# The HGRN scan stage rebuilt: block decays as one number each, values with channels on partitions, the root from a logarithm, and mem's attention moved among the value tiles

## The reference, cut to what matters

```python
q = silu(q); v = i                                   # 8 heads of 128
f = lb + (1 - lb) * sigmoid(z);  log_f = log(f);  k = 1 - f      # for zf and for zb
o = gla_chunked(q, k_f, v, lf_f) + flip(gla_chunked(flip(q), flip(k_b), flip(v), flip(lf_b)))
o = rmsnorm(o, norm_g.reshape(8, 128)) * silu(gate)
return concatenate([o, memory_cross_attn(xq, mem_kv)]) @ w_out
# gla: out[t] = sum over s <= t of (q[t] . (k[s] * exp(sum of log_f over s+1..t))) v[s]
```

## Time and profile before

| what | us |
|---|---|
| median of 3 runs (lowest to highest) | 1550.86 (1549.63 to 1552.31) |
| the profiled execution's own time | 1549.63 |
| its span in the trace | 1548.3 |
| HGRN stage in it, from PE's first value matmul (1074.04) to ACT's first step of the norm behind it (1338.55) | 264.5 |
| PE busy over the span | 1451.5 |
| DVE, ACT, POOL busy over the span | 984.0, 724.6, 206.2 |

### The profile page before, as it was taken

The page is one execution under the profiler, slowest core; times in us unless marked ns, Lnnn a source line. Parts: engine busy times, 40 slices in busy tenths (PEclk is TensorE's granted clock), DMA queues, the critical chain, the costliest instruction groups (busy, mean ns, idle before and its releaser), DMA issues.

```text
span 1548.3 us, 23402 instructions
## 1 busy us (share of the span) xinstructions
PE 1451.5 (94%) x9687; PEld 1282.6 (83%) x9687; DVE 984.0 (64%) x1697; ACT 724.6 (47%) x1041; POOL 206.2 (13%) x170
## 2 busy tenths in 40 slices
PE   7899999999999999999999999999987847799998
PEld 5887799999977999977667999996986746699997
DVE  5754576767756766673561666555599986365555
ACT  4434255554523554534453544454565643454443
POOL 2661300000000000027225000000000132400000
PEclk8999999999989999999999999999989858999999
DMA  8322155554442655525123456553532221355551
GB/s 306 139 101 109 55 218 191 215 184 180 191 163 104 222 191 218 191 109 184 62 82 109 168 186 218 191 182 140 198 124 93 82 96 41 136 191 181 193 194 73
DMA packets 36570, 240.42 MB, mean 155 GB/s; under 512 B 3880, under 2 KB 6256, under 8 KB 8944
## 3 DMA queue, kind: packets, MB, share of 16 engines
q1 hardware_dynamic: 36464, 238.92, 42.6%
HBM read 236.27 MB, written 2.64 MB: 154 GB/s over the span
## 4 chain that ended last, share of the span: by engine, by line
PE 80%; DVE 11%; ACT 5%; POOL 2%; issue 1%; DMA 0%; SPq 0%; DVEq 0%; ACTq 0%
PE ps L356 23%; PE ps L323 14%; PE ps L324 14%; PE ps L325 14%; DVE wlo L280 2%; PE ps L478 2%; PE ps L485 2%; POOL wlo L273 1%; DVE gb L1916 1%; PE ps L1568 1%; ACT whi L265 1%; PE ps L807 1%; PE ps L1582 1%; ACT gb L1825 1%; DVE ar L1953 1%
## 5 line engine op out<-in xcount | busy, mean ns | idle before, releaser
L323 PE MATMUL ps<-XS,whi 128*128 128x256 f32 x2088 | 603.6, 289 | 15.3 <-DVE XS L531 4.9
L324 PE MATMUL ps<-XS,whi 128*128 128x256 f32 x2088 | 599.1, 287 | 0.0
L325 PE MATMUL ps<-XS,wlo 128*128 128x256 f32 x2088 | 598.3, 287 | 0.0
L280 DVE TENSOR_TENSOR wlo<-raw,whi 128x2048 fp32r<-128x2048 f32 x168 | 383.8, 2287 | 162.0 <-ACT whi L265 161.8
L265 ACT ACTIVATE whi<-raw 128x2048 fp32r<-128x2048 f32 x204 | 388.5, 1907 | 136.4 <-PE ps L356 98.3
L323 PEld LDWEIGHTS ps<-XS,whi 128*128 128x128 f32 x2088 | 410.1, 196 | 21.4 <-issue 10.3
L324 PEld LDWEIGHTS ps<-XS,whi 128*128 128x128 f32 x2088 | 409.9, 196 | 1.6 <-issue 0.2
L325 PEld LDWEIGHTS ps<-XS,wlo 128*128 128x128 f32 x2088 | 409.2, 196 | 0.0
L356 PE MATMUL ps<-whi,MS 128*128 128x512 f32 x1024 | 291.0, 391 | 5.8 <-POOL wlo L273 5.2
L273 POOL TENSOR_TENSOR wlo<-raw,whi 128x512 fp32r<-128x512 f32 x142 | 189.3, 1367 | 587.3 <-ACT whi L265 587.3
L356 PEld LDWEIGHTS ps<-whi,MS 128*128 128x128 f32 x1024 | 189.2, 188 | 46.0 <-POOL wlo L273 6.4
(11 more groups left out here) (248 smaller groups left out, 1432.7 us busy)
## 6 DMA issues: line engine op xcount, KB each, us to landing
raw<-in_up SPq DMA_DIRECT2D x88, 1024.0 KB, 4.8
raw<-in_down SPq DMA_DIRECT2D x44, 1024.0 KB, 4.8
raw<-in_hg_t SPq DMA_DIRECT2D x16, 1024.0 KB, 4.8
raw<-in_od_t SPq DMA_DIRECT2D x8, 1024.0 KB, 5.0
raw<-in_ev_a SPq DMA_DIRECT2D x7, 1024.0 KB, 8.2
raw<-in_wa_o SPq DMA_DIRECT2D x6, 1024.0 KB, 4.8
raw<-in_hg_o SPq DMA_DIRECT2D x6, 1024.0 KB, 4.8
raw<-in_ev_o SPq DMA_DIRECT2D x4, 1024.0 KB, 7.1
```

The lines of the kernel that those rows point to most:

```text
L280: ve.tensor_tensor(lo[:, 0:w], r[:, 0:w], hi[:, 0:w].bitcast(F32), ALU.subtract).then_inc(w_lo_v)
L323: pe.matmul(d, hi[:, c], S[:, k, 0:256], start=(k == 0), stop=False)
L324: pe.matmul(d, hi[:, c], S[:, k, 256:512], start=False, stop=False)
L325: last = pe.matmul(d, lo[:, c], S[:, k, 0:256], start=False, stop=(k == 7))
```

## The change

Every part of it is in the HGRN stage.

- **Decays.** Only the 32-blocks keep their own exponentials: DVE takes two scans that restart at each block (`M32`, `CS`), one reduction for the sum of log f over each block, one scan of these 16 sums and four small subtractions that give one number for each block and level (`AA`, 48 columns). One subtraction of 512 columns makes `DD`. ACT takes exp(DD), exp(-DD) and exp(AA). The factors of the coarser levels are the factors of the 32-blocks times one number for each block (`X1_`, `X2_`, `X3_`).
- **Gates.** The logarithm takes scale and bias in the ACT instruction (`lf` straight from `SZ`), and k is not formed: a second sigmoid with the sign turned (`SN`) times a column.
- **Values** come with channels on partitions: two matmuls of 256 columns. ACT squares them, PE sums over partitions by a matmul with ones (`squares_pe`), ACT takes exp(-0.5 ln(.)) (`root_act`), DVE multiplies. Newton, the scaling, the turn on PE and the accumulated squares go.
- **Mem's attention** moves to the front: its query tiles come second and third, and its steps stand between the value tiles and the first heads. Its probabilities now lie in `gb`.
- **Low parts.** POOL makes every second `hg_t` tile (q and gate), `hg_x`, and `hg_o` tiles 0, 2 and 4. DVE makes the z tiles, `hg_v` and `hg_o` 1, 3 and 5.
- **Output.** The order is `hg_o` 4, 5 (mem's rows), 0, 1, 2, 3. The first four stand inside iterations 8 and 9.
- **Loop.** It runs over n from 0 to 10: projections of head n, factors of head n-1, values of head n-2, root of head n-3.

```diff
@@ tiles
-    add("hg_v", 4, ends=[1, 1, 1, 2])
+    add("hg_v", 1)
+    add("hg_x", 2)
+    add("hg_v", 3, at=1, ends=[1, 1, 2], key="hg_w")
     add("hg_t", 16)
-    add("hg_x", 2)
-    add("hg_o", 6, ends=[1, 1, 1, 1, 0, 4])
+    add("hg_o", 2, at=4)
+    add("hg_o", 4, ends=[1, 1, 0, 4], key="hg_p")
@@ who makes the low part
-POOLT = [_t[0] in ("ev_v", "ev_b", "ev_c", "ev_o", "hg_x", "hg_o") or _t[0][:2] == "wa"
-         or (_t[0] == "ev_a" and _t[1] > 1) for _t in SCHED]
+POOLT = [_t[0] in ("ev_v", "ev_b", "ev_c", "ev_o", "hg_x") or _t[0][:2] == "wa"
+         or (_t[0] == "ev_a" and _t[1] > 1) or (_t[0] == "hg_t" and _t[1] % 2 == 1)
+         or (_t[0] == "hg_o" and _t[1] % 2 == 0) for _t in SCHED]
@@ PE, values and squares
+            for sb_ in range(2):
+                last = pe.matmul(HVAL[:, 0:256], HV[:, sb_, 128 * h:128 * h + 128], HS[h % 2][:, 256 * sb_:256 * sb_ + 256],
+                                 start=(sb_ == 0), stop=(sb_ == 1))
             last.then_inc(h_va.up())
+        def squares_pe(h):
+            pe.wait_ge(h_sr.sem, h + 1)
+            if h:
+                pe.wait_ge(h_rs.sem, h)
+            pe.matmul(HSUM[:, 0:256], C("ones")[:, 0:128], SR, start=True, stop=True).then_inc(h_su.up())
@@ ACT, iteration n
+                    nc.scalar.preload_act_table_set("natural_log_exp_and_others")
+                    ac.wait_ge(h_sz.sem, h + 1)
...
+                        ins = ac.activation(lf[:, d, 1:257], SZ[:, 256 * d:256 * d + 256], ACT.Ln, bias=lm[:, o:o + 1],
+                                            scale=e0[:, o:o + 1])
...
+                    act_weights(min(at_z(n + 1), LAST[6]))
...
+                    ac.activation(PP, DD, ACT.Exp).then_inc(h_de.up())
+                    ac.activation(NN, DD, ACT.Exp, scale=-1.0).then_inc(h_de.up())
+                    ac.activation(EG, AA, ACT.Exp).then_inc(h_de.up())
...
+                    root_act(n - 3)
...
+                    ac.activation(SZ, BZ[n % 2][:, :], ACT.Sigmoid)
+                    ac.activation(SN[n % 2], BZ[n % 2][:, :], ACT.Sigmoid, scale=-1.0).then_inc(h_sz.up())
...
+                act_weights(min(at_q(n + 1), LAST[6]))
...
+                    ac.activation(SR, HVAL[:, 0:256], ACT.Square).then_inc(h_sr.up())
...
+                    ac.wait_ge(h_on.sem, n - 2)
+                    ms_high(n - 3, ON[(n - 3) % 2])
...
+                    ac.activation(SQ, BQ[n % 2][:, :], ACT.Sigmoid).then_inc(h_sq.up())
@@ DVE, iteration n
+                    gates_dve(n - 1)
+                    differences_dve(n - 1)
...
+                    masked_dve(n - 2)
+                dve_weights(min(at_z(n + 1), LAST[6]))
...
+                    factors_dve(n - 1)
...
+                    ve.wait_ge(h_rs.sem, h + 1)
+                    ve.wait_ge(h_ug.sem, h + 1)
+                    ve.tensor_tensor(ON[h % 2], UG[h % 2], RS, ALU.mult).then_inc(h_on.up())
...
+                    ve.wait_ge(h_sr.sem, h + 1)
+                    ve.scalar_tensor_tensor(UG[h % 2], HVAL[:, 0:256], col("bng", h), GT[h % 2], ALU.mult,
+                                            ALU.mult).then_inc(h_ug.up())
...
+                    ms_low(n - 3, ON[(n - 3) % 2])
```

More of the change, by code:

```diff
@@ L1686, in program @@
+        UG = [R(256) for _ in range(2)]
         ON = [R(256) for _ in range(2)]
[L1687 to L1695, removed]
+        AA, EG, MM = R(48), R(48), R(16)
+        M32, M8, EPS = R(256), R(16), R(1)
@@ L1714, in hgrn_pe @@
             filled(5)
[L1715 to L1718, removed]
+            project(hx, bank[4], xs_both(6 - 1))
+            project(hx + 1, bank[5])
+            accumulate([hw], XS, [2, 3], 1024, accs, no_wait, False, False)
+            for i in range(2):
+                top_pe(i, HB, xS, lambda o, i=i: cross_score(X1, o, i))
+            accumulate([hw + 1], XS, [4, 5], 1024, accs, no_wait, False, False)
@@ L1767, in scores_pe @@
                 pe.wait_ge(h_mk.sem, 2 * h)
-            qf, kf, qb, kb = (F0[:, 256 * i:256 * i + 256] for i in range(4))
+            else:
+                pe.wait_ge(ms_lo.sem, H0 + 4)
+            qf, kb, kf, qb = FL[:, 0:256], FL[:, 256:512], FE[:, 0:256], FE[:, 256:512]
             for tile in range(2):
@@ L1774, in scores_pe @@
                     pe.matmul(DIAG[r, 32 * tile:32 * tile + 32], kb[:, o:o + 32], qb[:, o:o + 32], start=True, stop=True)
-            for lev in range(1, 4):
-                half_ = 16 << lev
-                xf_ = F1[:, 512 * (lev - 1):512 * (lev - 1) + 256]
-                xb_ = F1[:, 512 * (lev - 1) + 256:512 * lev]
+            for i in range(4):
+                near, far = slice(32 * i, 32 * i + 32), slice(64 * i + 32, 64 * i + 64)
+                tile, r = i // 2, 64 * (i % 2)
+                c = 256 * tile + 64 * i
+                pe.matmul(MAIN[r:r + 32, c + 32:c + 64], X1_[:, near], qf[:, far], start=True, stop=True)
+                pe.matmul(MAIN[r + 32:r + 64, c:c + 32], kb[:, far], X1_[:, 128 + 32 * i:160 + 32 * i], start=True, stop=True)
+            for half_, X in ((64, X2_), (128, X3_)):
                 for o in range(0, 256, 2 * half_):
                     L_, R_ = slice(o, o + half_), slice(o + half_, o + 2 * half_)
-                    for x, ks, qs in ((xf_, L_, R_), (xb_, R_, L_)):
+                    for x, ks, qs in ((X[:, 0:256], L_, R_), (X[:, 256:512], R_, L_)):
                         tile, r = ks.start // 128, ks.start % 128
@@ L1789, in values_pe @@
             if h:
-                pe.wait_ge(h_on.sem, h)
-            s = HS[h % 2]
-            for tt in range(2):
-                for sb_ in range(2):
-                    last = pe.matmul(HVAL[:, 128 * tt:128 * tt + 128], s[:, 256 * sb_ + 128 * tt:256 * sb_ + 128 * tt + 128],
-                                     HV[:, sb_, 128 * h:128 * h + 128], start=(sb_ == 0), stop=(sb_ == 1))
-            last.then_inc(h_va.up())
+                pe.wait_ge(h_sr.sem, h)
+                pe.wait_ge(h_ug.sem, h)
@@ L1893, in hgrn_dve @@
             ve.wait_ge(dv.sem, dv.n)
-            ve.tensor_scalar(e0, lm, -1.0, 1.0, ALU.mult, ALU.add).then_inc(dv.up())
-            ve.wait_ge(dv.sem, dv.n)
-            dve_weights(ht + 3)
-            lf = LF.rearrange("p (d t) -> p d t", d=2)
-            for n in range(-1, 10):
+            ve.tensor_scalar(e0, lm, -1.0, 1.0, ALU.mult, ALU.add).then_inc(l_e.up())
+            dve_weights(hw + 1)
+            top_dve(0, HB, xS, hNM, csegs)
+            top_dve(1, HB, xS, hNM, csegs)
+            dve_weights(hw + 2)
@@ L2024, in hgrn_sp @@
         def hgrn_sp():
[L2025 removed]
+            sp_weights(LAST[6] - 2)
             next_gain_sp(6)
```

438 lines of the change are left out of this document (216 added, 222 removed).

## The result

The changed kernel takes 1506.99 us (median; 1505.85 to 1511.69) where the kernel before takes 1551.59 (1549.63 to 1556.52). The ratio is 0.9714, with a 95% interval of 0.9683 to 0.9745: 44.6 us faster. The forecast was 1488, 62.4 us faster.

The account below looks back on a forecast made before the run. DVE was taken to bound the heads at 21.0 us each. Stage end 1183.2 + 6 x 15.5 = 1276.2, against 1338.55, saves 62.4: 1549.63 - 62.4 = 1487.2 profiled, median 1488; range 1479 to 1508.

Parts of the forecast that it names:

- the end point: Stage end: last product before taken at 1338.55, new end forecast at 1276.2, so 62.4 us saved.
- PE's prices: PE's work per head: two projected tiles at 5.79 plus 2.75 for scores, values and squares, 14.3 us.
- DVE's sum: DVE's work per head: 12.1 us in place of 21.0, so DVE no longer bounds by its sum.
- Table switches: ACT's two table loads per head, 1.28 us each, with no drain added; the skill's drain would give 1497.
- Front: Before the first head cycle: 66.8 us of PE work, a 3.3 us pause, 1.0 for lower clock; cycle begins at 1146.1.
- Mem's softmax: Mem's attention beside value tiles: no cost on PE; rival that it doesn't hide: 9.5 us more, 1498, chance 0.07.
- one such wait for each head on a loop, 1.1: DVE beside POOL's q-tile low part: one wait of 1.1 us per head, lengthening the cycle from 14.3 to 15.4.
- loop 2: From one q sigmoid to the next over DVE: 13.7 us, 14.1 with eight changes of engine.
- The clock: Rival in the heads: shorter pauses keep PE at the lower clock, cycle 28.6 us, time up to 1593; chance 0.03.
- the port bounds: Rival in the heads: all four POOL operations per head delay DVE by 1.1 us each, time 1508; chance 0.13.
- C: Cycle of one head in the loop: forecast 15.5 us, with six such cycles in the stage.

Follow-up runs that it names:

- e2: The changed kernel with all low parts of the stage (q tiles, hg_x, hg_o) on DVE, none on POOL: 1474.97 us, ratio 0.9495.
- e5: The changed kernel with only the hg_o low parts moved from POOL to DVE: 1494.93 us, ratio 0.964.
- e9: The changed kernel with POOL's low parts of the stage cut into pieces of 128 columns in place of 512: 1500.53 us, ratio 0.9653.
- e4: The kernel before, with only the q tiles' low parts (every second hg_t) moved to POOL: 1567.29 us, ratio 1.009.
- e1: The changed kernel with the q tiles' low parts back on DVE, hg_x and hg_o as in the changed kernel: 1496.61 us, ratio 0.9617.

## Why the prediction was right or wrong

- **Direction and range: right, the range by luck at its edge.** DVE bounded the heads at 21.0; with Newton, its gaps and 7.8 of DVE's 19.6 us of work a head gone (2.2 of the 7.8 to POOL) they take 18.0 in the mean, and mem's attention left the end. But 1507 is 1 us inside the range, and it is inside because two errors of opposite sign met: the stage was 22.7 us longer than its sum, and the end point gave 5.4 of that back. With the end point read rightly the range would have ended near 1503.
- **PE's prices: right to 2%.** A head costs 14.60 (e2), forecast 14.3; values, squares and scores together take 3.0, not 2.75.
- **DVE's sum: right.** Forecast 12.1; in the steady cycle DVE is busy 15.55, less 3.25 and 0.46 of waits 11.8, and in e2 28.06 / 2 less the q tile's 2.2 is 11.8 as well. The new small instructions cost 0.16 and less.
- **Table switches: right, without a drain.** In ACT's timeline of the changed kernel the load starts 0.02 us behind the sigmoid and the logarithm 1.30 us later:

```profile
1200.15 0.58 ACT L1905 ACTIVATE ar<-ps 128x512 f32<-128x512 f32 x1
1200.75 1.28 ACT L1861 ACT_TABLE_LOAD   x1
1202.05 1.09 ACT L1867 ACTIVATE ar<-ar,lb 128x256 f32<-128x256 f32 x2
```

- **Front: right in the sum.** The pause is there, 3.16 us for 3.3. The clock behind it was put at 1.0 and took 2.5 in the profiled execution (two query tiles in 14.11 us, 11.58 in e5); e2, which has a pause of 0.42 and no slow clock, needs 67.4 where the forecast's PE work was 66.8. Mem's softmax hides, as forecast; PE waits for nothing of it. The pause in PE's timeline of the changed kernel:

```profile
1084.86 0.55 PE L326 MATMUL ps<-XS,whi 128*128 128x256 f32 x1 [3.16 <-issue]
```

- **The term that failed: "one such wait for each head on a loop, 1.1".** The size of a wait was right (1.07), their number wrong: three in a steady head, five in the first of the six cycles and six on the way to the end of the last. The reason given, "each time that DVE pauses, POOL gets in", read the earlier trace rows too narrowly. There POOL met DVE in Newton's gaps, and I took the gap for the condition. In e9 and in the changed kernel POOL gets in between instructions that stand back to back. The steady loop is the prediction's loop 2, 14.1, with 3.25 in place of 1.1: 17.35 against 17.24 measured. The waits fall on the factors and the root's product, the place that it named.
- **Not seen: POOL's output tile in iteration 7.** The sum priced iterations 7 to 9 as the others or as bare PE work. The order showed POOL two tiles in a row there, and the second met the differences ahead of the mask. e5 gives its price: 13.8 us of stage, of which 2.5 are the front's clock, so some 11.
- **The clock** was a rival only as a lasting fall. In the changed kernel it fell for a part of a cycle behind each pause of 2.7 us and more: in the six cycles PE waited 15.0 us in all, and the other 5.6 of 108.2 - 6 x 14.6 = 20.6 are slow matmuls. Behind its pauses of 0.5 to 1.95 it stayed at 1.00.
- **The end point: wrong by 5.4**, as shown above, in the other direction, so the total looks better than the working was.
- **The rival "the port bounds"** (C = 18.7, 1508; its own sum, 1488 + 6 x 3.2, gives 1507) is nearest to what happened, with a mean C of 18.0. It was given 0.13. It priced four waits in every head; the steady heads have three on the loop, and the rest came from the long cycles and from iteration 8, which it left at 13.8. From PE's end to PE's end its stage of 221.4 would have given about 1502, so that its time is met is luck too. Its argument against itself, that mask and gates read PSUM, is right (the mask keeps 0.68) and too weak: there were enough others.

The Trainium skill (SBUF — State Buffer, Who interferes with whom) says that a DVE instruction with two SBUF inputs and a GpSimd instruction that reads SBUF exclude each other, the later one waiting out the whole other instruction. By that rule, the traces agree for these three: two-input forms are hit (1.22 for 0.16), PSUM readers are not (0.68), and the wait goes with the length of POOL's instruction (0.26, 0.54, 1.07, 2.17). It also exempts reductions; the reduction of e9 keeps its 0.62 while POOL works. The prediction had cited this rule and then applied it once a head. The two lines of e4 that read SBUF once and wait show that such a list of two-input instructions is not complete.

## What to carry to other kernels

Before giving POOL a share of elementwise work, list DVE's instructions of that stretch that read SBUF twice, and look at small ones that read it once as well (e4): as long as POOL works, count up to one wait per POOL instruction that stands beside them, each nearly as long as that instruction, and compare it with the work saved. At 512 and 1024 columns nearly every POOL instruction of a steady head cost such a wait, at 256 three or four of eight, at 128 seven of sixteen. Here it took 3.25 us from DVE to save it 2.2, and giving everything back to DVE was worth 32 us. When several loops are within a few tenths of each other, every such microsecond reaches the end; and when something is moved forward, ask what other work it lets fill the gaps at the end, since that was worth more than the moved work itself.

## What the runs showed of the hardware that was not expected

- POOL gets between DVE instructions that follow each other without a gap; an 8-column subtraction took 1.22 us beside POOL's 512-column instructions and 0.42 beside its 128-column ones.
- The clock behind the same pause differs between executions. The pause of 3.16 us at the front stands in the changed kernel, in e1 and in e5, and the clock fell behind it in the first alone; the two query tiles behind it, first of the changed kernel and then of e5:

```profile
1084.86:1096.44 11.58, 11.58 (x75) 11.58 (x76) 7.73 (x8) 2.94 (x3) 4.83 (x4) 0.75 0.75 272
```

```profile
1083.22:1094.80 11.58, 11.58 (x97) 11.58 (x97) 9.49 (x8) 2.95 (x3) 4.90 (x4) 1.00 0.73 272
```

In the first PE was for a part of the 11.58 us at the lower of its two levels (1.2 against 2.4 GHz) and did 75 matmuls, in the second it stayed at the higher and did 97. Why the two differ stays open.
